# Two query tiles of each attention head turned by VectorE and DMA, and value products one head period later

## What is computed

```python
qx = mla_queries(hx, w_dq, g_q, w_uq, cos, sin)       # 16 heads, 64 + 32 (rotary) wide
kx, vx = mla_keys_values(hx, w_dkv, g_kv, w_uk, w_uv, cos, sin)
kc, vc = mla_keys_values(hc, ...)                      # of 256 context tokens
ox = block_attention(qx, concat([kc, kx]), concat([vc, vx]))
x = x + g1 * (ox @ w_o)
```

## Time and profile before

| | us |
|---|---|
| runs of the kernel | 1644.77, 1644.83, 1646.06; median 1644.83 |
| span of the profiled execution | 1645.5 |
| granted TensorE clock, mean of the span | 0.997 |
| attention stage, first transpose to end of last value product (112.92 to 316.76) | 203.84 |
| TensorE busy in it | 202.52 |
| VectorE, ScalarE, GpSimd busy in it | 148.22, 151.84, 139.04 |
| DMA traffic in it | 116 GB/s on average |

### The profile page before, as it was taken

The page is one execution under the profiler, slowest core; times in us unless marked ns, Lnnn a source line. Parts: engine busy times, 40 slices in busy tenths (PEclk is TensorE's granted clock), DMA queues, the critical chain, the costliest instruction groups (busy, mean ns, idle before and its releaser), DMA issues.

```text
span 1645.5 us, 24018 instructions
## 1 busy us (share of the span) xinstructions
PE 1633.9 (99%) x8950; PEld 1364.2 (83%) x8950; DVE 1043.6 (63%) x1537; ACT 571.0 (35%) x1017; POOL 1026.5 (62%) x656
## 2 busy tenths in 40 slices
PE   9999999999999999999999999999999999999998
PEld 7887778798888888889887798888888898888887
DVE  3567777677877865635487566655558359746173
ACT  3467777633233232203344243222222121123111
POOL 3455766656666766575579456666676645567663
PEclk9999999999999999999999999999999999999999
DMA  9234335232269863435322233344434253223332
GB/s 371 87 90 129 111 106 165 79 93 96 89 211 320 298 225 103 141 137 172 120 90 65 77 99 102 125 156 140 153 106 143 97 214 120 65 84 103 91 101 90
DMA packets 59095, 220.61 MB, mean 134 GB/s; under 512 B 6849, under 2 KB 9153, under 8 KB 55682
## 3 DMA queue, kind: packets, MB, share of 16 engines
q1 hardware_dynamic: 53826, 204.96, 38.2%
q10 hardware_dynamic: 5184, 14.49, 2.3%
HBM read 201.07 MB, written 14.16 MB: 131 GB/s over the span
## 4 chain that ended last, share of the span: by engine, by line
PE 95%; DVE 4%; ACT 0%; issue 0%; DMA 0%; DVEq 0%; SPq 0%; ACTq 0%
PE PS L2444 28%; PE PS L2446 28%; PE PS L2445 28%; PE PS L2821 3%; PE PS L2783 2%; PE PS L1012 1%; PE PS L2430 1%; PE PS L1785 1%; PE PS L2595 1%; DVE SC L3572 0%; DVE WA L1990 0%; PE PS L1791 0%; DVE MR L3522 0%; PE PS L2720 0%; PE PS L2721 0%
## 5 line engine op out<-in xcount | busy, mean ns | idle before, releaser
L2354 POOL TENSOR_TENSOR WL<-RAW,WH 128x1024 fp32r<-128x1024 f32 (+3 forms) x211 | 542.8, 2572 | 17.6
L2444 PE MATMUL PS<-HH,WH 128*128 128x512 f32 (+1 forms) x1340 | 507.5, 379 | 0.0
L2446 PE MATMUL PS<-HH,WL 128*128 128x512 f32 (+1 forms) x1340 | 502.9, 375 | 0.0
L2445 PE MATMUL PS<-HL,WH 128*128 128x512 f32 (+1 forms) x1340 | 502.9, 375 | 0.0
L2351 POOL TENSOR_SCALAR WH<-RAW 128x1024 fp32r<-128x1024 f32 (+3 forms) x211 | 239.4, 1134 | 287.8 <-PE PS L2446 276.5
L2444 PEld LDWEIGHTS PS<-HH,WH 128*128 128x128 f32 x1340 | 252.2, 188 | 50.7 <-issue 6.2
L2446 PEld LDWEIGHTS PS<-HH,WL 128*128 128x128 f32 x1340 | 252.2, 188 | 45.9
L2445 PEld LDWEIGHTS PS<-HL,WH 128*128 128x128 f32 x1340 | 252.3, 188 | 43.9
L2379 POOL TENSOR_SCALAR PR<-PR,SC 128x768 f32<-128x768 f32 x47 | 107.3, 2292 | 66.7 <-DVE SC L3579 66.3
L2444 PE MATMUL PS<-HIDH,WH 128*128 128x512 f32 (+1 forms) x396 | 145.3, 367 | 0.0
L2445 PE MATMUL PS<-HIDL,WH 128*128 128x512 f32 (+1 forms) x396 | 144.8, 366 | 0.0
(11 more groups left out here) (532 smaller groups left out, 2894.6 us busy)
## 6 DMA issues: line engine op xcount, KB each, us to landing
RAW<-in_wup SPq DMA_DIRECT2D x88, 512.0 KB, 3.6
MRF<-in_modw SPq DMA_DIRECT2D x52, 512.0 KB, 4.8
RAW<-in_wdn SPq DMA_DIRECT2D x32, 704.0 KB, 4.1
MR<-in_modw SPq DMA_DIRECT2D x28, 512.0 KB, 3.6
RAW<-in_whin SPq DMA_DIRECT2D x24, 512.0 KB, 3.5
MK<-in_modk SPq DMA_DIRECT2D x8, 1024.0 KB, 10.9
RAW<-in_wo SPq DMA_DIRECT2D x8, 512.0 KB, 4.2
hy_hs<-HST ACTq DMA_DIRECT2D x4, 1024.0 KB, 4.0
```

The source lines that it names most:

```text
L2354: pool.tensor_tensor(WL[s][:, 0:n], raw[:, 0:n], WH[s][:, 0:n].bitcast(F32), ALU.subtract).then_inc(tile_split, 1)
L2444: pe.matmul(out, wh, xh, start=first, stop=False)
L2445: pe.matmul(out, wh, xl, start=False, stop=False)
L2446: return pe.matmul(out, wl, xh, start=False, stop=last)
```

## The change

Of each head's four query tiles (heads 0 to 14), the first two are no longer transposed by TensorE. The exponential of these tiles reads the scores in another order (every fourth key first) and writes them straight. When they are normalised, VectorE turns each 32x32 block of such a tile in place (`block_turn`, 128x768). SyncE writes both tiles to DRAM (`blocks_out`, 384 KB each) and reads them back in one DMA (`blocks_in`, 768 KB, in pieces of 192 numbers) with the keys on the partitions, into `PB`. TensorE transposes the other two tiles (`turn`, twelve transposes a head in place of 24), and ScalarE copies them out in three copies of 128x512.

The value product of head h moves behind the end of its period, to the start of the next one; the scores of the head after next follow right behind it, where eight transposes stood ahead of them before. It takes half of its moving operand from `PB` and half from `PT`. The two groups of transposes of the first four key tiles stand behind the second score tile, the last behind the fourth (and the keys). Head 15 is transposed as before, in the tail. The outputs of all heads but the last go to bank 7.

Of the modulation rows, four come ahead of head 0, two or so in head 0, in odd heads and in heads 13 and 14; 24 are taken in this stage in place of 28, and the feed-forward layer takes the other four in one more pair of tiles (`EARLY`, `LATE`). SyncE's loop over head pairs becomes one over heads, with the block DMAs of a head first. Some semaphores are shared between uses that follow each other (`low_rank`, `side_in`, `sq_add`); the transfers and instructions are the same there. The removed lines of the functions below can be seen in the kernel above.

```diff
-EARLY, LATE, LAST_ROWS = 28, 11, 88
+EARLY, LATE, LAST_ROWS = 24, 10, 88
+BLOCKED = 2
+PRE_ROWS = 4
+LAST_HEAD = HEADS - 1
...
-        PT = r.put("PT", [P, 6, L])
+        PB = r.put("PB", [P, BLOCKED, 4, 6, 32])
+        PT = r.put("PT", [P, 6, P * (4 - BLOCKED)])
+        PT_LAST = Region(pt_at).put("PT_LAST", [P, 6, L])
...
+        d_blocks = nc.dram_tensor("pr_blocks", (2, BLOCKED, P, LK), F32).ap()
...
+        def outputs(h, half):
+return PS[VH * half:VH * half + VH, 7 if h < LAST_HEAD else 3, 0:256]
...
+def blocks_out(h, qt):
+    sp.wait_ge(S["turned"], BLOCKED * h + qt + 1)
+    sp.dma_start(d_blocks[h % 2, qt, :, :], PR[h % 2][:, qt, :]).then_inc(S["blocks_out"], 16)
+def blocks_in(h):
+    sp.wait_ge(S["pv"], h + 1)
+    sp.wait_ge(S["blocks_out"], 16 * BLOCKED * (h + 1))
+    sp.dma_start(PB[:, :, :, :, :].rearrange("p i m t j -> p (i m) (t j)"),
+                 d_blocks[h % 2].rearrange("i (m k) (c x) -> (k c) (i m) x", m=4, c=4)
+                 ).then_inc(S["blocks_in"], 16)
...
+for r in range(PRE_ROWS):
+    mod_load(16 + r)
+    if r == 1:
+        head_weights(2)
...
+for h in range(LAST_HEAD):
+    for qt in range(BLOCKED):
+        blocks_out(h, qt)
+    blocks_in(h)
+    if h == 0:
+        two_rows(PRE_ROWS)
+    if h % 4 == 2 and h < 12:
+        rope_move(h + 2, 2)
+    elif h % 4 == 3 and h < 12:
+        rope_move(h + 3, 2)
+    if h % 2 == 0 and h < 10:
+        head_weights(h // 2 + 3)
+    elif h == 10 or h == 12:
+        ring("wo", a["wo"], h // 2 - 5)
+    if h % 2 == 0 and h < 14:
+        two_rows(PRE_ROWS + 2 + h)
+    elif h == 13:
+        sp.wait_ge(S["rope"], 512)
+        x_again(0)
+        two_rows(EARLY - 4)
+    elif h == 14:
+        two_rows(EARLY - 2)
...
+def turn(h, n):
+    if n == 0:
         pe.wait_ge(S["pnorm"], 3 * h + 2)
         if h == 0:
             pe.wait_ge(S["kready"], key_hi_at(0) + 2)
+        else:
+            pe.wait_ge(S["pt"], 4 * h + 1)
+    if n == 1 and h:
+        pe.wait_ge(S["olo"], 2 * h)
+    if n == 2:
+        pe.wait_ge(S["pt"], 4 * h + 2)
+    for kt in (2 * n, 2 * n + 1):
+        for qt in range(BLOCKED, 4):
+            q = (kt % 2) * 256 + (qt - BLOCKED) * P
+            m = pe.transpose(PS[:, 6 + n % 2, q:q + P], PR[h % 2][:, qt, kt * P:(kt + 1) * P], IDENT[:, :])
+    m.then_inc(S["s_tr"], 1)
...
 def value(h):
     if h == 0:
         pe.wait_ge(S["v_ev"], 12)
+    pe.wait_ge(S["pt"], 4 * h + 3)
     v = slice(VH * h, VH * h + VH)
+    pe.wait_ge(S["blocks_in"], 16 * (h + 1))
     for kt in range(6):
+        pe.wait_ge(S["pt"], 4 * h + kt // 2 + 2)
+        pe.matmul(outputs(h, 0).rearrange("p (i m j) -> p i m j", i=2, m=4), V[:, kt, v],
+                  PB[:, :, :, kt, :], start=kt == 0, stop=kt == 5)
+        m = pe.matmul(outputs(h, 1), V[:, kt, v], PT[:, kt, :], start=kt == 0, stop=kt == 5)
+    m.then_inc(S["pv"], 1)
...
+def chunk_between(h, n):
+    if h == 0:
+        project_pair(1, n)
+    elif h < 12 and h % 4 == 1:
+        project_rope((h + 3) // 4, n)
+    elif h < 12 and h % 4 == 2:
+        project_pair(h // 2 + 1, n)
+    elif h < 12 and h % 4 == 3 and n < 3:
+        project_pair(h // 2 + 2, n)
+    elif h <= 12 and h % 4 == 0 and n == 1:
+        project_pair(h // 2 + 1, 3)
+    elif h > 12 and n < 3:
+        wo_ahead(0, 3 * (h - 13) + n)
...
 def head(h):
+    early = h == 14
     if h:
+        value(h - 1)
+    if early:
+        chunk_between(h, 0)
     for qt in range(4):
+        score(h + 1, qt)
+        if qt == 3 and h < 14 and h % 2 == 0:
+            chunk_between(h, 3)
+            project_keys(h // 2 + 1)
+        elif qt < 3 or not early:
+            chunk_between(h, qt + early)
+        if qt == 1:
+            turn(h, 0)
+            turn(h, 1)
+    turn(h, 2)
...
+for h in range(LAST_HEAD):
     head(h)
+value(LAST_HEAD - 1)
+wo_ahead(1, 0)
+wo_ahead(1, 1)
+turn_last(0)
+turn_last(1)
+wo_ahead(1, 2)
+turn_last(2)
+turn_last(3)
+wo_ahead(1, 3)
+turn_last(4)
+turn_last(5)
+value_last()
...
     c = (4 * h + qt) % 8
     act.wait_ge(S["smax"], i * (4 * per) + (4 * h + qt + 1))
+    out, src = PR[h % 2][:, qt, :], wide(2 * (qt % 2), LK)
+    if qt < BLOCKED and (per or h < LAST_HEAD):
+        out, src = out.rearrange("p (c t j) -> p c t j", c=4, t=6), src.rearrange("p (t j c) -> p c t j", t=6, c=4)
+    act.activation(out, src, ACT.Exp, bias=NMX[:, c:c + 1], scale=1.0,
                    accum_out=SUMS[:, c:c + 1]).then_inc(S["sexp"], 1)
...
+def turn_copy(h, n, i=0, per=0):
+    act.wait_ge(S["s_tr"], i * (3 * per) + (3 * h + n + 1) + 1)
+    if n == 0:
         act.wait_ge(S["pv"], i * per + h + 1)
...
 def head(h, i=0, per=0):
+    first = h == 0 or h % 4 == 2 and h < 12
+    keys = h < 14 and h % 2 == 0
+    fourth = h % 4 == 0 and 0 < h <= 12
+    if h:
+        out_hi(h - 1, i, per)
+    if h % 4 == 0 and per:
+        mod_store(i)
+    if h % 4 == 3 and h < 12:
+        query_hi(h + 2, i, per)
+    exponential(h + 1, 0, i, per)
+    exponential(h + 1, 1, i, per)
     turn_copy(h, 0, i, per)
+    turn_copy(h, 1, i, per)
+    if fourth:
         query_hi(h + 2, i, per)
+    exponential(h + 1, 2, i, per)
+    if fourth:
+        query_hi(h + 3, i, per)
+    elif first:
+        query_hi(h + 2, i, per)
+    exponential(h + 1, 3, i, per)
+    if keys and not fourth:
         key_hi(h // 2 + 1, i, per)
+    turn_copy(h, 2, i, per)
+    if fourth:
+        key_hi(h // 2 + 1, i, per)
+    normalise(h + 1, i, per)
     if h % 4 == 1 and h < 12:
         rope_hi((h + 3) // 4, i, per)
...
+def block_turn(h, qt, i=0, per=0):
+    dve.wait_ge(S["pnorm"], i * (3 * per) + (3 * h + qt if h else qt + 1))
+    dve.transpose(PR[h % 2][:, qt, :], PR[h % 2][:, qt, :]).then_inc(S["turned"], 1)
...
+def head(h, i=0, per=0):
...
+    first = h == 0 or h % 4 == 2 and h < 12
+    fourth = h % 4 == 0 and 0 < h <= 12
+    rows = h == 0 or h % 2 or h == 14
+    maximum(h + 1, 0, i, per)
+    if h:
+        out_lo(h - 1, i, per)
+    maximum(h + 1, 1, i, per)
+    inverse_sum(h + 1, 0, i, per)
+    if h % 4 == 2 and h < 12:
+        rope_lo(h // 4 + 1, i, per)
+    if h % 4 == 3 and h < 12:
+        query_lo(h + 2, i, per)
+    if h % 2:
         row(0)
+    maximum(h + 1, 2, i, per)
+    inverse_sum(h + 1, 1, i, per)
+    if fourth:
+        query_lo(h + 2, i, per)
+    if rows and h % 2 == 0:
         row(0)
+    maximum(h + 1, 3, i, per)
+    if fourth:
+        first_keys(h // 2 + 1, i, per)
+    inverse_sum(h + 1, 2, i, per)
+    if h < 14:
+        block_turn(h + 1, 0, i, per)
     if h % 4 == 1 and h < 12:
         rope((h + 3) // 4, i, per)
+    if fourth:
+        query_lo(h + 3, i, per)
+    elif first:
         query_lo(h + 2, i, per)
+    if rows and h != 0:
+        row(1)
+    inverse_sum(h + 1, 3, i, per)
+    if h < 14 and not fourth:
+        block_turn(h + 1, 1, i, per)
     if h < 14 and h % 2 == 0:
         key_lo(h // 2 + 1, i, per)
+    if fourth:
+        block_turn(h + 1, 1, i, per)
+    if h == 14:
+        row(2)
     if h == 0:
         query_lo(3)
+        row(1)
```

More of the change, by code:

```diff
@@ L2863, in head @@
-                if h < 14 and h % 2 == 0:
-                    project_keys(h // 2 + 1)
-                value(h)
-                if h == 14:
-                    wo_ahead(0, 6)
+                    score(h + 1, qt)
[7 more added lines that the diff above has]
+                        turn(h, 1)
@@ L3121, in head @@
             def head(h, i=0, per=0):
-                turn_copy(h, 0, i, per)
-                for kt in range(1, 6):
-                    turn_copy(h, kt, i, per)
-                    if kt == 1 and h % 4 == 3 and h < 12:
-                        query_hi(h + 2, i, per)
-                    if kt < (4 if h == 14 else 5) and h < 15:
-                        exponential(h + 1, kt - 1, i, per)
-                    if kt in (2, 3) and h % 4 == 0 and 0 < h <= 12:
-                        query_hi(h + kt, i, per)
@@ L3132, in head @@
-                if h == 14:
-                    exponential(15, 3)
-                first = h == 0 or h % 4 == 2 and h < 12
-                if first:
-                    query_hi(h + 2, i, per)
-                if h < 15:
-                    normalise(h + 1, i, per)
-                if h < 14 and h % 2 == 0:
+                first = h == 0 or h % 4 == 2 and h < 12
[3 more added lines that the diff above has]
+                    out_hi(h - 1, i, per)
@@ L3175, in _ @@
                     head(h, i, 4)
-            for h in range(13, 16):
+            for h in range(13, LAST_HEAD):
                 head(h)
+            out_hi(LAST_HEAD - 1)
+            for kt in range(6):
+                turn_copy_last(kt)
+            out_hi(LAST_HEAD)
             def squares(stage, j):
@@ L3593, in row @@
+            def head(h, i=0, per=0):
                 def row(k):
-                    if rows:
-                        if k == 0 and h % 2 == 0 and h:
-                            dve.wait_ge(S["modx"], i * (per // 2) + h // 2)
```

(19 more changed lines are left out.)

262 lines of the change are left out of this document (94 added, 168 removed).

## The result

The changed kernel takes 1674.64 us (median of 4 runs, 1671.32 to 1675.82), the kernel before 1645.44 on the same chip: ratio 1.0172 [1.0158, 1.0186]: 1.7% slower, well clear of the noise, though under the 2% from which a change is called slower here. The forecast was 1637.0, the range 1627 to 1651. The profiled execution has a span of 1669.5 us, 24.0 more than that of before, where the medians differ by 29.2. Part of that is which executions the profiles caught. The time of a run is 1.8 to 2.0 us above its span in all runs of the kernel before, so its span of 1645.5 belongs to an execution of some 1647.4 us, 2 above the median (the text above takes the span for the time); the profile after is that of the fastest of its four (1671.32). What follows explains the 24.0 us between these two.

The account below looks back on a forecast made before the run. TensorE's own instructions were taken to bound the kernel (52.02 of 52.29 us a cycle). Its -20.0 us plus 12.2 us of waits, (a) to (d), gave -7.8: 1637.7 us from 1645.5, 1637.0 as a median, range 1627 to 1651.

Parts of the forecast that it names:

- (d): Start of the attention stage: two modulation rows between head 0's maxima make a projection 1.3 us late.
- TensorE's own work: Attention stage: fewer transposes and fewer returns from them take 20.0 us off TensorE.
- (a): Keys in heads 4, 8, 12 wait for the third tile's exponential: stall 1.5 us, 1.0 more each, 3.0 in all.
- (b): First scores of a new key pair wait for VectorE behind heads 4, 8, 12: 1.2 us each, 3.6 in all.
- (c): Blocks' DRAM write and read take 7.8 us (bounds 6.0 to 12); value products wait only where slack is short.
- Head 1 and head 14: Stalls in the way through DRAM: 1.9 us from head 1's writes behind a waiting load, 0.8 in head 14's period.
- What lies behind the attention stage moves as a whole: Output projection and everything after it keep their length: no gain or loss there.
- transposes' 15.9 us: Heads 0 to 14 each lose 12 of 24 transposes: 180 x 0.0885 us less on TensorE.
- returns: TensorE pays 0.09 us per switch back from transposes; three fewer per head, 45 in all, save 4.1 us.
- rival B: A block turn costs two passes, near 1.6 us, so VectorE can't fill its waits: 1651 us; chance 0.10.
- rival D: Strided PSUM reads double the exponential, so score tiles wait for banks: 1644 us, no change; chance 0.03.
- Rival C: The way through DRAM takes near 12 us, from 1,024 pieces a head and 512 KB rows: 1652 us; chance 0.16.

Follow-up runs that it names:

- e3: The changed kernel with the DRAM round trip left out for heads 1 to 14, which use head 0's blocks; 1652.36 us, ratio 1.0034.
- e1: The changed kernel with head weights and modulation rows issued ahead of the rope moves in heads 2, 6 and 10; 1663.54 us, ratio 1.0099.
- e11: e9 with the output projection's last eight small VectorE operations split over two residuals, and both modulation rows loaded in odd heads; 1644.75 us, ratio 0.9993.
- e8: The changed kernel with 79 extra value matmuls ahead of the long block waits, alternating between both output halves; 1667.76 us, ratio 1.0129.
- e7: e6 with VectorE's small 16-column operations moved from the output projection to the feed-forward stage's first periods; 1664.27 us, ratio 1.0102.
- e6: e1 plus late rows' loads behind block writes, one row per head, and new keys and last query ahead of block turns (heads 4, 8, 12); 1653.12 us.
- e9: e6 with first block turn ahead of key copy (heads 4, 8, 12), input's first half behind head 14's block read, head 13's row earlier; 1648.18 us.
- e12: e11 with the DRAM round trip made for head 0 alone; 1642.26 us, ratio 0.9975.
- e4: The changed kernel with extra value matmuls ahead of the long block waits, all on one output half; 1680.31 us, ratio 1.0202.

## Why the prediction was wrong

The forecast was a span of 1637.7, the profile shows 1669.5: 31.8 us to explain (by the medians, 1674.64 against 1637.0, it is 37.6). By the windows:

| term | forecast | measured | off by |
|---|---|---|---|
| start of the stage (d) | +1.3 | -1.5 | -2.8 |
| TensorE's own work | -20.0 | -15.7 | +4.3 |
| other engines in (a), (b) and elsewhere | +6.6 | +12.6 | +6.0 |
| the way through DRAM, (c) and the rest of it | +4.3 | +22.3 | +18.0 |
| output projection | 0 | +6.2 | +6.2 |
| what follows | 0 | +0.1 | +0.1 |

(TensorE's work: busy 199.78 to 184.10 in e3. Other engines: idle time 1.32 to 13.90 in e3. The way: after less e3; this has the waits and the low clock behind them.)

**The step that failed first** is the sentence in (c) "Elsewhere rope moves, head weights and rows have their releases before the next head's turns". I asked when the instructions in front of the block writes leave the queue, and not when their bytes have landed. They do leave it in time, at 154.2 in head 2, one instruction ahead of the writes; their 1.6 MB are then in front of the writes' 0.77 MB. A write takes 2.3 us with nothing ahead, which is the 2.4 that I took, and 7.7 to 8.8 with that; the read takes 5.0 (5.2 in the sum). From the issue of the writes to value product 3 it is 14.3 us, where the sum had 7.8. That sum was right for a free queue, and the waits of 3.0, 4.0 and 3.0 us in heads 3, 7 and 11, where it had none, are the bytes'. The Trainium skill (DMA: Bandwidth & Descriptors, section "Queues, rings and completion order") says that an issuing engine has one ring on each of the DMA engines and that each consumes it in order; the landing times agree, and e1 and e11 show that order decides.

**The clock** was missing from the sum altogether. Each wait of 3 to 5 us was followed by a value product at a granted clock of 0.50 to 0.64. e8 prices it at 6.9 us. The forecast had two waits there (heads 1 and 14, 1.9 and 0.8 us) and charged them with their length alone.

**Head 1 and head 14** had their mechanism right: a block write stands behind a load that waits for VectorE's last row. In head 0 the turns are done at 123.4, the writes go out at 127.84. Forecast 1.9 and 0.8 us, measured 4.8 and 3.0: I took no time for the row of 512 KB that the same wait puts right in front of the writes (issued at 127.5, and at 310.3 in head 14). Behind it they took 4.8 to 5.5 us where the sum had 2.4. What the 1 MB of the input, issued at 303.55, adds in head 14 is not shown by itself; it landed 6.9 us later, about when the writes went out.

**"What lies behind the attention stage moves as a whole"** failed by 6.2 us. VectorE's small operations between residuals have no fixed duration; one of 16 columns took 0.17 us or 2.23, and I take it that the phase decides whether they meet a GpSimd split. e7 shows that these operations hold up the residuals. That their meeting the splits is chance of the phase is argued from the timelines; e6 and e9, with the same order of VectorE's work there and waits of 4.8 and 0 us for residuals, speak for it (e9 moves a load of the input, too).

**(a) and (b)** were the right places with a size near the right one: key projection and third tile wait 1.6 us in all, counted from start to start (forecast 1.5), the scores behind the new keys 1.7 (forecast 1.2), three times each. What I had not seen are shorter waits in other heads: the same bank wait of 0.5 us in heads 2, 6 and 10, the value products' own waits for the last copy (0.2 to 0.5, and 1.3 for that of head 14), and 0.65 in head 2 (all in e3). They make most of the 6.0.

**TensorE** was mis-sized. A cycle of four heads without the trip (e12, from value product 3 to value product 7) has 47.6 us of TensorE (before 52.02). The forecast said 47.0, but its own -20.0 us over fifteen heads gives 46.7 for a cycle:

```profile
163.03:212.19 49.16, 47.61 (x301) 36.58 (x300) 41.20 (x70) 33.69 (x67) 35.76 (x17) 1.00 0.29 85
```

The transposes' 15.9 us are there; of the 4.1 us for returns little is left. The first score behind a value product starts its successor 1.16 us later and not 1.04, and the switch from transposes to a value product takes 0.53 where four transposes to a score take 0.35. The length of the cycle in e12, 49.16 us, is what the sum without the trip gives (about 49).

**What held**: 204 transposes; the block turn at 0.96 us (0.85 to 0.95 expected, 0.90 in the sum), so rival B's 1.6 is refuted, and it agrees with the one element per cycle per lane of the Trainium skill (Vector Engine (DVE) Microarchitecture Reference, section 3.8), an estimated 0.8 us and a fixed part; the exponentials, strided and straight together, at 897 to 910 ns and 903 in the mean, as before, so rival D is too; the value product with runs of 32 at 2.74 us, as before. Their rows, by line (busy us, mean ns):

```profile
L3679 DVE STREAM_TRANSPOSE PR<-PR 128x768 f32<-128x768 f32 x30 | 28.6, 956 | 0.0
```

```profile
L3156 ACT ACTIVATE PR<-PS,SC 128x768 f32<-128x768 f32 x64 | 57.8, 903 | 53.2 <-DVE SC L3657 52.6
```

VectorE's 41.20 us in the cycle are near the 41.5 of the sum. Rival C had the right sign; of its two reasons, the pieces of 768 bytes are not one (a read lands in 5.0 us) and the rows of 512 KB are. The waits came in five heads, not in each. (d) came about as forecast: from the first score tile of head 0 to the stage it is 16.18 us (95.24 to 111.42), where it was 15.13 (97.79 to 112.92), so 1.05 more and not 1.3. The -2.8 of the table is mostly from ahead of that tile, in code that the change leaves alone; the stage starts anywhere from 111.4 to 115.7 us in the later runs.

**What is left of the gain.** With all repairs (e11) the kernel takes what it took before: 0.9993 [0.9983, 1.0002]. TensorE is busy 16.2 us less in the stage (199.78 to 183.54) and stands still 7.3 us more, so that the stage is 8.9 us shorter (192.17 against 201.10); the output projection is 4.6 us longer (47.13 against 42.53). That leaves 4.3 us in these two profiles, of which the medians show 1.1. Of the 4.6 us, TensorE waits 2.2 for the low half of the last outputs and 1.9 for residuals. Without the trip (e12) it is 0.25% faster, which no correct order of these transfers is shown to reach.

## What to carry to other kernels

Where a new transfer enters an in-order queue, add up the bytes ahead of it at the time when it is issued, and not only the instructions; then do the same for every transfer that a repair moves behind them (the rope moves of e1). Price a wait of TensorE of a few microseconds with what follows it at the lower clock (here 6.9 us behind waits of 3.0 to 4.8 us in five heads). An engine that loses its cover (52.02 of 52.29 us) shows half a dozen waits of 0.2 to 0.5 us that no earlier profile could list: look for them in each head of a cycle, not only in the fullest.

## What was not expected of the hardware

Value matmuls that write different halves of PSUM's partitions run side by side. A matmul in float32 leaves two records here (a value product: 12 matmuls, 24 records). In e4, with all extra ones on one half, 37 records take 8.20 us; in e8, by turns on both, 36 take 4.11:

```profile
135.50 8.20 PE L2861 MATMUL PS<-PT,V 128*64 128x256 f32 x37
```

```profile
134.14 4.11 PE L2861 MATMUL PS<-PT,V 128*64 128x256 f32 x36
```

That is 0.44 us for a matmul alone on its half and, in the value product (2.74 us for 12), 0.46 for two on both (as in the second row), so the second is nearly free. The Trainium skill (TensorEngine Tiling (Array Packing), section "When to Use Tiling") gives a factor of two for a stationary operand of up to 64 columns; the two rows agree.
